# Weight loads moved to ScalarE's queue: twenty gate tiles, and half of each load of U

## What is computed

```python
z = rms_norm(x) @ w_in                      # q, k, v, pooling input p, gate logits gl (4096 columns)
gates = sigmoid(gl + b_gate)
# prompt attention over 512 tokens; sample attention over 1024 paged keys and values per sequence
merged = gates[:, :, 0] * (attention @ w_attn_branch) + gates[:, :, 1] * (pooled @ w_pool_branch)
h = x + merged @ w_out
# expert mixer: 8 heads, 16 of 16384 experts each per token
act  = gelu(hn @ u[experts]); out = (gate * act) @ v[experts]     # hn = rms_norm(h)
```

## Time and profile before

| | |
|---|---|
| median of 3 runs | 4253.15 us (4247.58 to 4256.39) |
| the profiled execution | 4267.19 us, its span 4264.7 us |
| PE busy | 4140.2 us (97%) |
| DVE busy | 2820.8 us (66%) |
| ACT busy | 1125.0 us (26%) |
| POOL busy | 1351.2 us (32%) |
| moved by DMA | 968.41 MB, mean 227 GB/s |

### The profile page before, as it was taken

How to read it: one execution, slowest core, us unless ns; L and a number is a source line. 1 busy time by engine, 2 the same in 40 slices (tenths; PEclk the granted TensorE clock), 3 DMA queues, 4 the chain that set the end, 5 groups by cost and what they waited for, 6 DMA issues and landing times.

```text
span 4264.7 us, 65385 instructions
## 1 busy us (share of the span) xinstructions
PE 4140.2 (97%) x27173; PEld 3887.8 (91%) x27173; DVE 2820.8 (66%) x3997; ACT 1125.0 (26%) x1420; POOL 1351.2 (32%) x1067
## 2 busy tenths in 40 slices
PE   8999999999999999999999999999999999999998
PEld 7999888888999999899999888888889999999998
DVE  3241465442434356798898777777778888888887
ACT  3212352222212121222222222222222222222224
POOL 1001000112000000055677677776123343333320
PEclk9999999999999999999999999999999999999999
DMA  6433227996466643367789999999889999999983
GB/s 199 116 104 99 88 64 209 260 265 211 151 203 209 198 96 75 78 131 148 189 203 288 264 267 266 267 271 264 255 325 361 356 353 354 352 365 352 360 337 129
DMA packets 590151, 968.41 MB, mean 227 GB/s; under 512 B 103953, under 2 KB 398865, under 8 KB 555800
## 3 DMA queue, kind: packets, MB, share of 16 engines
q1 hardware_dynamic: 453600, 553.50, 45.7%
q0 software_dynamic: 131072, 400.85, 28.3%
q10 hardware_dynamic: 5184, 9.90, 0.7%
HBM read 873.63 MB, written 85.95 MB: 225 GB/s over the span
## 4 chain that ended last, share of the span: by engine, by line
PE 74%; DMA 14%; DVE 6%; SPq 3%; issue 1%; ACT 1%; another core or an unknown queue 0%; DVEq 0%; ACTq 0%
PE pair L2017 27%; PE pair L2431 25%; PE pair L2369 14%; DMA w_raw<-in_peer_u_dram 12%; PE quad L2017 2%; DVE turned L1695 2%; DMA k_page<-in_cache_k_dram 2%; PE quad L2413 1%; SPq L576 1%; DVE w_lo L1700 1%; PE quad L1987 1%; SPq L637 1%; PE pair L2055 1%; PE quad L2342 0%; ACT w_hi L947 0%
## 5 line engine op out<-in xcount | busy, mean ns | idle before, releaser
L2369 PE MATMUL pair<-act_hi,w_hi 128*128 128x448 f32 x2048 | 759.2, 371 | 41.4 <-DVE w_lo L1700 41.2
L2369 PE MATMUL pair<-act_lo,w_hi 128*128 128x448 f32 x2048 | 754.9, 369 | 0.0
L2369 PE MATMUL pair<-act_hi,w_lo 128*128 128x448 f32 x2048 | 754.8, 369 | 0.0
L841 POOL DMA_INDIRECT gmat_dram<-g_val,g_idx x384 | 645.9, 1682 | 269.9 <-DVE g_val L1775 118.6
L2017 PE MATMUL pair<-act_hi,w_hi 128*128 128x288 f32 x3264 | 718.1, 302 | 11.7 <-DVE act_lo L1386 3.6
L2017 PE MATMUL pair<-act_hi,w_lo 128*128 128x288 f32 x3264 | 701.1, 297 | 0.0
L2017 PE MATMUL pair<-act_lo,w_hi 128*128 128x288 f32 x3264 | 700.2, 296 | 0.0
L2431 PE MATMUL pair<-wx_hi,v_hi 128*128 128x384 f32 x2016 | 679.2, 337 | 7.0 <-issue 4.7
L2431 PE MATMUL pair<-wx_lo,v_hi 128*128 128x384 f32 x2016 | 674.8, 335 | 1.7 <-issue 1.7
L2431 PE MATMUL pair<-wx_hi,v_lo 128*128 128x384 f32 x2016 | 674.9, 335 | 0.0
L1333 DVE TENSOR_TENSOR w_lo<-w_raw,w_hi 128x2048 fp32r<-128x2048 f32 x102 | 233.2, 2286 | 653.7 <-ACT w_hi L947 653.4
(11 more groups left out here) (337 smaller groups left out, 5326.1 us busy)
## 6 DMA issues: line engine op xcount, KB each, us to landing
w_raw<-in_peer_u_dram SPq DMA_DIRECT2D x512, 256.0 KB
v_raw<-in_peer_v_dram SPq DMA_DIRECT2D x256, 512.0 KB
w_raw<-in_w_in_dram SPq DMA_DIRECT2D x64, 1024.0 KB
k_page<-in_cache_k_dram SPq DMA_DIRECT2D x256, 128.0 KB
gelu_dram<-tmp SPq DMA_DIRECT2D x128, 224.0 KB
gmat_dram<-zeros SPq DMA_DIRECT2D x48, 512.0 KB, 7.0
a_back<-gelu_dram SPq DMA_DIRECT2D x128, 192.0 KB
g_back<-gmat_dram SPq DMA_DIRECT2D x64, 384.0 KB
```

Of the source, the lines that this page charges most:

```text
L841: pool.indirect_dma_start(out=gmat_cells, out_offset=bass.IndirectOffsetOnAxis(ap=g_idx[:, b, n:n + 1], axis=0), in_=g_val[:, b, n:n + 1], ...
L2369: op = m_(pair[0][:, n % 2, 0:TU], w[n % 2][:, k, :], x[:, k, 0:TU], start=(k == 0 and i == 0), stop=(k == KD - 1 and i == 2))
```

## The change

Two groups of weight loads are issued by ScalarE in place of SyncE. Tiles 44 to 63 of `w_in` are loaded by ScalarE's new `load_gate`, in slots 3, 7, ... 79, ahead of that slot's `gate_sigmoid`. For U tiles 3 to 127 (U_SHARED = 3) SyncE issues the first and second quarter, and ScalarE the third and fourth, right behind its rounding of the second half of the tile two before. Buffers, semaphores and counts stay as they were; a form of `load_u` for a tile number in a register, which nothing calls, is gone.

```diff
+U_SHARED = 3
@@ for all engines
+        def u_part(n, s, q):
+            dst = w_raw[s][quadrant(q), :, :].rearrange("p k c -> p (k c)").rearrange("p (e d) -> p e d", e=NQ)
+            return dst, u_tiles[:, :, n, q * KD * QR:(q + 1) * KD * QR]
@@ SyncE
             for g in range(2, G_U):
-                load_tile(g)
+                if not T_G + 12 <= g < N_IN:
+                    load_tile(g)
@@ SyncE, load_u(n, s)
-                for q in range(NQ):
-                    ds = slice(q * KD * QR, (q + 1) * KD * QR)
-                    src = u_tiles[:, :, n, ds] if isinstance(n, int) else ...
-                    sp.dma_start(w_raw[s][quadrant(q), :, :]..., src).then_inc(raw_in[s], 16)
+                for q in range(NQ if n < U_SHARED else NQ // 2):
+                    sp.dma_start(*u_part(n, s, q)).then_inc(raw_in[s], 16)
@@ ScalarE
+            def load_gate(g):
+                act.wait_ge(lo_done, g - 1)
+                for src, ps, ks in ring_source(g):
+                    act.dma_start(w_raw[g % 2][ps, ks, :], src).then_inc(raw_in[g % 2], 16)
@@ ScalarE, for i in range(SLOTS)
                 if i % 4 == 3:
+                    if T_G + 12 + i // 4 < N_IN:
+                        load_gate(T_G + 12 + i // 4)
                     gate_sigmoid(9 + i // 4)
@@ ScalarE, u_high(n, s), for i in range(2)
                     a.copy(w_hi[s][:, 8 * i:8 * i + 8, :], turned[i][:, :, :]).then_inc(u_hi, 1)
+                    if i == 1 and U_SHARED <= n + 2 < N_U:
+                        for quarter in range(NQ // 2, NQ):
+                            act.dma_start(*u_part(n + 2, n % 2, quarter)).then_inc(raw_in[n % 2], 16)
```

More of the change, by code:

```diff
@@ L633, in load_u @@
             def load_u(n, s):
-                for q in range(NQ):
-                    ds = slice(q * KD * QR, (q + 1) * KD * QR)
-                    src = u_tiles[:, :, n, ds] if isinstance(n, int) else u_tiles[:, :, bass.ds(n, 1), ds].rearrange("c e a d -> c e (a d)")
-                    sp.dma_start(w_raw[s][quadrant(q), :, :].rearrange("p k c -> p (k c)").rearrange("p (e d) -> p e d", e=NQ),
-                                 src).then_inc(raw_in[s], 16)
+                for q in range(NQ if n < U_SHARED else NQ // 2):
+                    sp.dma_start(*u_part(n, s, q)).then_inc(raw_in[s], 16)
             def store_gelu(n):
```

## The result

The kernel after takes 4188.07 us (median of 4 runs, 4183.41 to 4191.69) against 4250.36 us for the kernel before in the same comparison (4 runs, 4242.20 to 4256.39): 0.9854 of it, with an interval from 0.9833 to 0.9875, so 62 us less. The profiled execution took 4185.87 us with a span of 4183.8, 80.9 us less than the 4264.7 of the profile before. The 19 us between the two differences come from the profile of before, which stood 17 us above its own median (4267.19 against 4250.36). So sizes taken between the two profiles are somewhat large, and the medians of the experiments decide where they differ.

The account below looks back on a forecast made before the run. TensorE, busy 97% of the span, was taken as the bound, with U and key-page loads on its path. 4267.2 us less 32 and 4 is 4231, times 0.9967 for the median: 4217 us, range 4193 to 4260.

Parts of the forecast that it names:

- rival 1: Both stretches: engines are full, service order doesn't matter, nothing moves; 4253 us within 8, chance 0.16.
- the term of 32 us: U stage: half of each U load in ScalarE's queue lets U land earlier and gaps fill, 32 us gained.
- I take the rate, as the bytes must be moved, and three quarters of it: U stage: 10.0 us a tile by rate gives 42 us; three quarters, for ScalarE's later start, gives 32 us.
- by the share: U stage: pace sized by DMA share, 10.63 x 0.99 / 1.08 = 9.75 us a tile, a gain of 59 us.
- the gaps close: U stage: earlier U loads and turns send requests earlier, so rows fill DMA gaps; 10.63 to 10.0 or 9.75 us a tile.
- Rows early, U late: U stage: U's loads are served too late (158.9 us of VectorE waiting), gathered rows too early.
- the term of 4 us: Page stretch: with gate tiles in ScalarE's queue, key pages behind them are no longer late, 4 us gained.
- Order can give 5 us, and bytes keep the other 26: Page stretch: of 31 us lost in pace, 5 come from order; 26 stay, bound by bytes at 267 GB/s.
- The added wait of `load_gate`: Gate tiles: ScalarE's wait for VectorE's low part is hidden by TensorE's lead; taken at nothing, bounds 0 and 27 us.
- ScalarE's issues: U stage: two more issues a tile, 109 us in all, cost nothing as ScalarE is idle for most of it.
- Rival 2: U stage: ScalarE's half lands too late, a pair loses 2.4 us, 4333 us; chance 0.12 with other losses over 0.2%.
- Rival 3: All gaps close in both stages, 61 + 5 us, TensorE's pace throughout: 4188 us; chance 0.06.

Follow-up runs that it names:

- experiment 2: Kernel before with only the U half of the change (third and fourth quarters on ScalarE), gate tiles on SyncE: 0.9879 of the kernel before.
- experiment 7: Kernel before, all U on SyncE's queue, third and fourth quarters held until ScalarE rounded the second half of the tile two before: 1.0017 of the kernel before.
- experiment 5: Kernel before with ScalarE rounding U tile n + 2 ahead of gelu n, loads and stores on SyncE as they were: 1.0021 of the kernel before.
- experiment 13: Kernel before with GpSimd gathering each row block two dots later, at most two in flight in place of four: 1.0130 of the kernel before.
- experiment 3: Kernel before with only the gelu store moved from SyncE to ScalarE, all of U staying on SyncE: 0.9939 of the kernel before.
- 6, all U on ScalarE: Kernel before with all four quarters of U tiles 3 to 127 on ScalarE behind its second rounding, gelu stores on SyncE: 0.9917 of the kernel before.
- experiment 9: Kernel before with each 256 KB quarter of U as two transfers of 128 KB, all in SyncE's queue: 0.9913 of the kernel before.
- 10, both: Kernel before with U's halves on SyncE and ScalarE, in transfers of 128 KB, gate tiles on SyncE: 0.9906 of the kernel before.
- experiment 11: Kernel before without the 384 scatters of gate values, all else in its queues of before: 0.9899 of the kernel before.
- experiment 1: Kernel before with only the gate-tile half of the change (`load_gate` on ScalarE), U staying on SyncE: 0.9957 of the kernel before.
- 14: Kernel before with only the gate tiles moved to ScalarE, each in four pieces of 256 KB: 0.9983 of the kernel before.
- 12: The whole change plus the third and fourth quarters of key pages 7 to 63 on ScalarE: 0.9910 of the kernel before.
- 8: Kernel before with gate tiles 44 to 63 loaded whole through GpSimd's queue, beside the value pages: 0.9996 of the kernel before.

## Why the prediction was right in direction and short in size

**Nothing moves (rival 1).** Wrong in both stretches. The Trainium skill, page "DMA: Bandwidth & Descriptors", section "Issuing engines are not separate DMA queues", from which that rival came, has it that issuing on several engines saves only the sequencers' time. For U the runs contradict this: with the same bytes, experiment 2 moved 293 GB/s where the kernel before moved 268, while SyncE's issues of U had only 6.5% of the chain before. For the key pages the rule fits better: what the chain lost there is mostly SyncE's issue time, though that had been 26.0% of the stretch.

**The U loads: the term of 32 us.** It came out at 57 us by the profiles and at 1.21% (0.86 to 1.56), some 52 us, by experiment 2. The mis-sized step is "I take the rate, as the bytes must be moved, and three quarters of it". The rate 284 GB/s was read from a stretch at TensorE's pace, where the bytes asked for were no more; it was not what the engines could do. And ScalarE's half cost nothing: its quarters landed in 8.5 us (median) of the 10.1 that it had, so the quarter taken off for lateness was not due. Measured, the pace went to 9.75, the figure worked out "by the share".

**Its mechanism, "the gaps close".** The gaps did close: of tiles 54 to 118, 4 of 625 microseconds were below a share of 0.7, where it had been 50 of 682, and the share rose from 1.00 to 1.07 (2400 to 2900 us). As the cause of the gain this is not enough: experiment 7 closed all gaps and experiment 5 most of them (8 microseconds below 0.7 left), and neither gained. The DMA view from 2400 to 2900 us (packets, MB, share of 16 engines), of the kernel before:

```profile
q1 hardware_dynamic: 33668, 59.81, 51.5%
q0 software_dynamic: 33618, 72.85, 47.9%
```

of the kernel with the late half in one queue (experiment 7):

```profile
q0 software_dynamic: 33627, 73.39, 59.1%
q1 hardware_dynamic: 33632, 59.72, 50.3%
```

and of the kernel after:

```profile
q0 software_dynamic: 37049, 80.32, 55.9%
q1 hardware_dynamic: 22327, 38.98, 30.8%
q10 hardware_dynamic: 14822, 27.00, 20.4%
```

The share times 16 engines times 500 us, over the bytes, is the engine time of a KB. For SyncE's and ScalarE's queues together it is 0.515 x 8000 / 59.81 = 68.9 ns before, 67.4 in experiment 7, and 0.512 x 8000 / 65.98 = 62.1 after. All kernels by the same sum:

| kernel | U pace, us | GB/s | DMA share | ns per KB, SyncE's and ScalarE's | ns per KB, GpSimd's | ns per KB, all three |
|---|---|---|---|---|---|---|
| 13, rows held back | 10.96 | 260 | 0.99 | 69.0 | 53.9 | 60.7 |
| 5, rounding first | 10.70 | 267 | 1.06 | 69.1 | 59.4 | 63.7 |
| before | 10.66 | 266 | 1.00 | 68.9 | 52.6 | 59.9 |
| 7, late half, one queue | 10.63 | 267 | 1.10 | 67.4 | 64.4 | 65.8 |
| 3, store on ScalarE | 10.02 | 284 | 1.07 | 66.5 | 55.3 | 60.3 |
| 6, all U on ScalarE | 9.82 | 291 | 1.09 | 62.3 | 58.2 | 60.1 |
| 9, small transfers | 9.79 | 290 | 1.08 | 65.3 | 55.3 | 59.7 |
| after | 9.76 | 293 | 1.07 | 62.1 | 55.7 | 58.6 |
| 2, U alone | 9.74 | 293 | 1.08 | 62.4 | 56.2 | 59.0 |
| 10, both | 9.73 | 291 | 1.09 | 60.4 | 59.2 | 59.7 |
| 11, no scatters | 9.73 | 294 | 1.03 | 68.7 | 45.7 | 56.1 |

The rate is 16 times the share over the last column, so a kernel can be slow in two ways. The kernel before and 13 have the low share, at 60 to 61 ns. Experiments 5 and 7 filled the gaps, and a KB took 64 to 66 ns instead. The fast ones have the higher share and stay at 56 to 60. From before to after, most of the gain in rate is the share (1.07 of 1.10). The time that a packet takes has its waiting inside it, so these figures order the kernels and do not give the cause. No single column does it either. In experiment 3 SyncE's queue carries U alone:

```profile
q1 hardware_dynamic: 28455, 51.82, 45.8%
q10 hardware_dynamic: 7197, 11.47, 6.8%
```

By the same sum that is 70.7 ns per KB for U and 47.4 for the stores. U's packets are no quicker there than in experiment 7, with 67.4 for both kinds together, and the pace is 0.6 us better.

So three kinds of edit were shown to give back all or most of U's pace: another queue for U or for the store (2, 3, 6), smaller transfers (9), and no scatters (11). The held rounding alone (5) is excluded as the cause. The moment of issue is made unlikely by 3 and 6, and rows served ahead of need take part (13), though holding them back costs more. Why the gaps fill without dearer packets in these and not in 5 and 7 stays open; that the scatters' small packets, which share GpSimd's queue with the gathers, hold up one hardware queue more than two would fit, but is not shown. The Trainium skill's rule of turns ("Queues, rings and completion order" on the same page) is not contradicted: three queues served in turn would also favour U. By itself it doesn't explain experiment 9, where one queue did nearly as well.

**Rows early, U late.** Half right. After the change the first wait for rows shows (23.0 us), as the prediction allowed, and with two rows in flight in place of four VectorE never waited for U (experiment 13). But rows need their time: held back so far, they cost 55 us.

**The gate tiles: the term of 4 us.** It came out at 18.5 us by the profiles and 0.43% (0.11 to 0.74), some 18 us, by experiment 1. The step that failed is "Order can give 5 us, and bytes keep the other 26". It took the 267 GB/s at a share of 1.09 as what full engines move, and in the same stretch they then moved 285. The prediction had the better term in hand: it saw the page's four transfers take 5.21 us to issue, said that this would go, and gave it no price. On the chain those issues had 26.0% of the stretch, some 52 us, and have 6.2% in experiment 1, some 12; part of the difference is taken up by TensorE's matmuls, which then set the pace more often. Putting the tile elsewhere helps only if nothing that is needed soon then stands behind it. In ScalarE's queue as one transfer nothing does. In four pieces (14), or with page quarters in that queue (12), ScalarE's own issues are held, and the sigmoid with them. Why a transfer's issue is held by the ones ahead of it, and why GpSimd's queue (8) gave so little, is open.

**The added wait of `load_gate`,** taken at nothing with 27 us as the bound: right. ScalarE's queue and activations behind the worst of them, 818 to 825 us:

```profile
821.60 0.42 ACTq L1108 DMA_DIRECT2D w_raw<-in_w_in_dram  x1
822.11 1.28 ACT L1076 ACT_TABLE_LOAD   x1 [3.52 <-DVE w_lo L1348]
823.40 0.74 ACT L1076 ACTIVATE tmp<-pair,bgate_c 128x576 f32<-128x576 f32 x1
```

It held the sigmoid for 3.52 us, and once more for 2.9; TensorE was busy for 146.71 of 150 us in that stretch nevertheless.

**SyncE's queue.** The 5.21 us for four page issues behind a tile are gone; the same four now take 1.81. The 18.57 us of the last line cover sixteen issues and the waits between them:

```profile
786.05 1.81 SPq L582 DMA_DIRECT2D k_page<-in_cache_k_dram  x4
787.91 1.35 SPq L631 DMA_DIRECT2D gate_dram<-tmp  x1
790.47 18.57 SPq L582 DMA_DIRECT2D k_page<-in_cache_k_dram  x16
```

**ScalarE's issues,** 109 us taken at nothing: right, ScalarE waits for TensorE 494.6 us of the stretch. The pair that the earlier trace rows showed, now, SyncE's and ScalarE's queues and VectorE's turn:

```profile
2512.81 1.25 DVE L1710 STREAM_TRANSPOSE turned<-w_raw 128x1024 f32<-128x1024 f32 x1 [3.57 <-DMA w_raw<-in_peer_u_dram]
...
2514.76 0.55 ACT L1213 ACTIVATE tmp<-pair 128x448 f32<-128x448 f32 x1 [7.30 <-PE pair L2384]
...
2516.47 0.79 SPq L642 DMA_DIRECT2D w_raw<-in_peer_u_dram  x2
2516.48 1.05 ACT L1204 CAST w_hi<-turned 128x1024 fp32r<-128x1024 f32 x1 [0.23 <-DVE turned L1710]
2516.48 0.86 ACTq L1207 DMA_DIRECT2D w_raw<-in_peer_u_dram  x2
2517.30 0.44 SPq L646 DMA_DIRECT2D gelu_dram<-tmp  x1
```

The gelu waits for TensorE's 7.30 us again. SyncE's quarters go out when the turns are done (2512.81 on), and ScalarE's two in the same microsecond, not 5.7 us later: in this pair the turns are late and the roundings follow them at once. Over tiles 54 to 117 ScalarE's first issue comes 1.6 us after SyncE's in the mean. Rival 2 (4333) never came near.

**The rival on the other side and the spread.** Rival 3, given 0.06, was its time but only half its story: U's stage ran at nearly TensorE's pace, as it said, and the pages gave 18 us where it had 5. That the forecast's range was missed by only 5 us says little, since both terms were too small. A chance for "the engines can move more than the profile shows them moving" was missing, and they did so in both stretches.

## What to carry to other kernels

A DMA share near or above 1 says that packets are always under way, not that the engines move what they can: here a share of 1.07 went with 267 GB/s in one kernel and with 293 in another. Before calling a stretch bound by bytes, look for a stretch or a variant that moves more, and read in the chain how much of it is the issuing of transfers and how much their landing. Move the large or slow transfer to a queue in which nothing needed soon stands behind it. If that queue belongs to an engine that computes, watch what its own issues then take: four pieces cost ScalarE up to 9.9 us where the whole tile cost 0.4. And when a variant moves fewer bytes per second, ask first whether anything waited for bytes.

## What the runs showed of the hardware

- The share of the DMA engines and their rate part ways: 1.10 at 267 GB/s (experiment 7), 1.01 at 287 (experiment 11), 1.04 at 287 (after).
- With scatters and gathers beside it, a kernel with all of U and the stores in one hardware queue moved 266 GB/s with U in transfers of 256 KB and 290 with 128 KB (before and experiment 9, 2400 to 2900 us).
- An instruction that issues a transfer can hold its engine far longer than its usual 0.3 to 0.5 us when large transfers are ahead of it in the same queue: up to 6.83 us for one of 128 KB on SyncE behind the 1 MB tile, and 8.29 us for one piece of 256 KB on ScalarE behind other pieces (experiment 14).
- Four key-page issues took 1.81 us behind the tile of 745.68 us in the kernel before, and 4.58 to 8.32 us behind each of the next ten, among them the 5.21 of the earlier trace rows. So it is not the tile ahead alone that stretches an issue; what else it takes was not tried.

```profile
745.68 0.43 SPq L566 DMA_DIRECT2D w_raw<-in_w_in_dram  x1
748.07 1.81 SPq L576 DMA_DIRECT2D k_page<-in_cache_k_dram  x4
```
